# Two of the four loads of a conditioning quad moved behind the first result gathers, and its last products behind the second tile

## The reference, cut to what matters

```python
mod = (silu_c @ w_ada[i] + b_ada[i])[:, None, :]          # six vectors of 1024: shift, scale, gate, twice
h = _modulate(_rmsnorm(x, g_attn[i]), sh_a, sc_a)         # the same for the context with its own c
q, k, v = _split_qkv(h, w_qkv[i])
...
x = x + gt_a * (o @ w_o[i])
hf = _modulate(_rmsnorm(x, g_ffn[i]), sh_f, sc_f)
y = _hier_moe(tokens, w_group[i], ..., w_gate[i], w_up[i], w_down[i])
x = x + gt_f * y
```

## Time and profile before

| | us |
|---|---|
| median of 3 runs | 2221.47 |
| lowest and highest of them | 2219.11, 2228.01 |
| the profiled execution's own time | 2219.71 |
| its span in the trace | 2217.5 |
| PE busy | 1898.6 |
| DVE, ACT, POOL busy | 639.1, 400.2, 134.7 |

### The profile page before, as it was taken

How to read it: one execution, slowest core, us unless ns; L and a number is a source line. 1 busy time by engine, 2 the same in 40 slices (tenths; PEclk the granted TensorE clock), 3 DMA queues, 4 the chain that set the end, 5 groups by cost and what they waited for, 6 DMA issues and landing times.

```text
span 2217.5 us, 19432 instructions
## 1 busy us (share of the span) xinstructions
PE 1898.6 (86%) x7753; PEld 874.6 (39%) x7753; DVE 639.1 (29%) x1436; ACT 400.2 (18%) x821; POOL 134.7 (6%) x182
## 2 busy tenths in 40 slices
PE   6999968878787777886978778785999998999998
PEld 2445444323332323453323323331445553445553
DVE  1257553000000006765200000002353332362432
ACT  2146301000000012251100000001221220122220
POOL 1000002000000002001000000000100000100000
PEclk8999988999888988997999999997999999999999
DMA  9766248999999998424999999995733333533331
GB/s 368 291 259 251 99 161 334 427 427 426 427 426 424 426 397 331 160 98 151 410 426 427 427 426 427 424 419 202 247 116 123 123 114 131 200 115 115 114 114 57
DMA packets 103245, 612.13 MB, mean 276 GB/s; under 512 B 12986, under 2 KB 15306, under 8 KB 71788
## 3 DMA queue, kind: packets, MB, share of 16 engines
q1 hardware_dynamic: 85696, 572.52, 63.9%
q0 software_dynamic: 16880, 36.20, 4.8%
q10 hardware_dynamic: 576, 2.10, 0.3%
HBM read 597.43 MB, written 33.62 MB: 285 GB/s over the span
## 4 chain that ended last, share of the span: by engine, by line
PE 59%; DMA 31%; DVE 6%; ACT 1%; issue 1%; POOL 0%; SPq 0%; DVEq 0%; POOLq 0%; ACTq 0%
DMA ring<-in_w_up 24%; PE bank L706 14%; PE bank L925 12%; PE bank L786 6%; PE bank L939 5%; DMA big<-in_w_up 4%; PE bank L1003 4%; PE bank L1155 2%; PE bank L850 2%; PE bank L662 2%; PE bank L559 1%; PE bank L650 1%; PE bank L545 1%; DMA ring<-in_w_qkv 1%; DMA xl<-in_x 1%
## 5 line engine op out<-in xcount | busy, mean ns | idle before, releaser
L706 PE MATMUL bank<-ring,big 128*64 128x512 f32 x2656 | 742.5, 640 | 147.5 <-DMA ring<-in_w_gate 50.8
L706 PEld LDWEIGHTS bank<-ring,big 128*64 128x64 f32 x2656 | 247.3, 147 | 543.5 <-issue 512.0
L925 PE MATMUL bank<-ring,big 128*128 128x512 f32 (+1 forms) x640 | 282.2, 590 | 0.0
L706 PE MATMUL bank<-big 128*64 128x512 f32 x416 | 200.3, 638 | 19.6 <-DMA ring<-in_w_gate 9.5
L2010 DVE TENSOR_TENSOR big<-big,bank 128x512 f32<-128x512 f32 x32 | 22.0, 688 | 603.2 <-PE bank L706 603.2
L925 PEld LDWEIGHTS bank<-ring,big 128*128 128x128 f32 x640 | 117.5, 190 | 126.2 <-issue 126.1
L786 PE MATMUL bank<-ring,big 128*128 128x512 f32 x320 | 141.4, 601 | 2.5 <-ACT big L1199 2.1
L939 PE MATMUL bank<-ring,big 128*128 128x512 f32 x256 | 113.3, 601 | 1.7 <-issue 1.7
L1173 ACT ACTIVATE big<-bank 128x512 f32<-128x512 f32 (+1 forms) x86 | 48.2, 576 | 348.2 <-PE bank L786 101.7
L2016 DVE COPY big<-bank 128x512 f32<-128x512 f32 x32 | 22.1, 692 | 260.5 <-PE bank L706 260.5
L706 PEld LDWEIGHTS bank<-big 128*64 128x64 f32 x416 | 58.7, 146 | 84.2 <-issue 79.7
(11 more groups left out here) (371 smaller groups left out, 1824.6 us busy)
## 6 DMA issues: line engine op xcount, KB each, us to landing
ring<-in_w_up SPq DMA_DIRECT2D x56, 2048.0 KB, 23.4
ring<-in_w_down SPq DMA_DIRECT2D x56, 2048.0 KB, 24.7
ring<-in_w_gate SPq DMA_DIRECT2D x54, 2048.0 KB, 23.5
ring<-in_w_in SPq DMA_DIRECT2D x26, 2048.0 KB, 7.9
ring<-in_w_ada SPq DMA_DIRECT2D x24, 2048.0 KB, 7.8
big<-in_w_gate SPq DMA_DIRECT2D x10, 2048.0 KB, 21.2
big<-in_w_up SPq DMA_DIRECT2D x8, 2048.0 KB, 26.2
big<-in_w_down SPq DMA_DIRECT2D x8, 2048.0 KB, 24.3
```

The source lines that it names most:

```text
L706: ins = nc.tensor.matmul(bank[half * CAP:(half + 1) * CAP, :], lhs[:, k, half * CAP:(half + 1) * CAP], w[:, k * step + c0:k * step + c0 + ...
L925: ins = nc.tensor.matmul(u[:, 0:cols], HT2[:, k, tile * P:(tile + 1) * P], w[:, 0:KD * cols].rearrange("p (k n) -> p k n", k=KD)[:, k, :], ...
```

## The change

Three things move; nothing is added or left out.

- The list of weights: of layer 1's quad 4 only pieces 0 and 1 stand ahead of the three qkv pieces; pieces 2 and 3 stand behind them. SP has loads of two pieces instead of four to issue before it waits for tile 1's gathers (`s_yg[1]` at 32), and five instead of three behind that wait.
- PE: `fill_step(4, 4..7)`, half of the quad's products, moves from before tile 0's turn to behind `qkv_tile(1)`.
- DVE: `filled(4)` moves from between tile 1's modulation and the combining of tile 2 to the head of its work on tile 2.

```diff
-            put_quad(0 if layer == 0 else 4)
+            if layer == 0:
+                put_quad(0)
+            else:
+                put_quad(4, range(2))
             for c in range(3):
                 put(("qkv", layer, c), kmajor(t["w_qkv"][layer], c * 512, 512))
+            if layer == 1:
+                put_quad(4, range(2, 4))
...
-                for k in range(KD):
+                for k in range(4 if last else KD):
                     fill_step(4 if last else 0, k)
...
                     if tile < NT:
                         qkv_tile(tile)
+                    if last and tile == 1:
+                        for k in range(4, KD):
+                            fill_step(4, k)
                     if 0 <= tile - 2 < LAT:
                         qr_tile(tile - 2)
...
                     for tile in range(first, first + 2):
                         modulated_half(layer, tile)
-                    if last and first == 0:
-                        filled(4)
...
                 for tile in range(NT):
+                    if last and tile == 2:
+                        filled(4)
                     dve.wait_ge(s_outA, marks["qkv", layer, tile])
...
-                    for _ in range(4):
+                    for _ in range(2):
                         load(n)
                         n += 1
                     sp.wait_ge(s_yg[1], 32)
-                    for _ in range(3):
+                    for _ in range(5):
                         load(n)
                         n += 1
```

More of the change, by code:

```diff
@@ L373, in kmajor, with put_quad @@
             return w.rearrange("(k p) n -> p k n", p=P)[:, :, c0:c0 + n]
-        def put_quad(q):
+        def put_quad(q, items=range(KD // 2)):
             layer, c = QUADS[q]
-            for i in range(KD // 2):
+            for i in items:
                 put(("ada", q, i), kmajor(t["w_ada"][layer], c * 512, 4 * 512)[:, 2 * i:2 * i + 2, :])
```

## The result

The changed kernel took a median of 2227.01 us in 20 runs (2220.02 to 2234.76), the kernel before 2220.92 in 20 runs beside it (2216.52 to 2228.01). The ratio is 1.0024 [1.0014, 1.0033], or +5.3 us (+3.1 to +7.3): within the half per cent, but on the slow side of it. The forecast was 2222.9, a change of +1.4 us.

The account below looks back on a forecast made before the run. Bound before layer 1's attention: first the store and gathers, with nobody computing on the path, then PE with DVE touching it. -4.8 + 6.2 = +1.4 us on 2219.71 gives 2221.1, plus 1.8 a median of 2222.9; range 2217 to 2230.

Parts of the forecast that it names:

- The gain: Between layer 0's last store and layer 1's first gather: two withdrawn 2 MB loads give 4.8 us, bounded by 0 and 4.8.
- The first rival: At the last store: it is hardly helped, 0 to 2.4 us gained, median 2225.3 to 2227.7; chance 0.13.
- DVE's and PE's steps: Before quad 5's products: moved products cost DVE 3.3 us, `filled(4)` adds 2.9 us, together 6.2 us.
- The contact of the two engines at 919.3: At tile 2's rotated queries: DVE ends 0.05 us before PE needs its work, so neither has slack.
- Its distance stays: Second qkv piece, behind tile 1's gathers: its 17.90 us landing time was to stay unchanged.
- The clock: PE's clock falls at the wait before quad 5's products; price 1.7 us, median 2224.6; chance 0.12.
- Quad 5's last piece: Within quad 5's products: lands in time, 1.8 us to spare; rival has it late, +9.7 us, median 2231.2; chance 0.05.
- The bias: Quad 5's bias load on POOL: issue ends at 926.1, DVE wants it at 935.3, 9 us later.
- the three signs of being wrong: First gather moves under 3 us, PE waits within quad 5's products, or DVE's bias step is behind another wait.
- The sum: Stretch from last store to layer 1's attention: -4.8 + 6.2 = +1.4 us, median 2222.9; forecast chance 0.6.

Follow-up runs that it names:

- the small ones: 16 matmuls of 8 columns added ahead of quad 4's first half of products, against the changed kernel; ratio 1.002 [1.0005, 1.0034].

## Why the prediction was right in its range and short in its size

**The gain: right.** 4.8 us expected, 4.7 to 5.2 measured. From the store to the first gather it is 8.6 to 9.2 us in all five traces with the old loads, whatever the steps, and 3.8 to 4.5 in all nine without them. The store's own landing went from 8.27 to 3.55 us. So the loads held the store. The trace has a mark for each of the 16 shares in which a transfer lands, and it shows that a few shares made the difference, as the slow engines of the earlier trace rows would: in the kernel before 12 of the store's marks were set within 4.9 us and the last four only after 7.9 to 8.3; in the changed kernel 14 were set within 2.7. The Trainium skill, "DMA: Bandwidth & Descriptors", section "Queues, rings and completion order", has an engine's completion mark wait for its earlier writes. By that rule the store should land much sooner without the loads, and in this the trace agrees, with 3.55 us against 8.27. But the store did not wait for the loads' end: it landed at 835.4 and the second load only at 838.5, 21.0 us after its own issue at 817.4 (the 21.0 of the earlier trace rows is that load's alone). How the two shared the engines until then no run shows. The first rival, at most 2.4 us of gain, is out. The median alone could not have told: the measured 2227.0 lies within that rival's 2225.3 to 2227.7, and the stated range, 13 us wide, would have held a change of nothing as well. Being inside it says little; the times in the stretch are what bears the sum out or not.

**DVE's and PE's steps: right, 0.4 us small.** 6.2 expected, 61.43 - 54.79 = 6.64 measured: 3.06 for DVE's step instead of 2.9 (I left out the idle time at its edges), and 3.6 for PE's products, of which I had let 0.23 vanish in DVE's distance to the keys. The contact of the two engines at 919.3 was real: the wait is 3.02 us with and without PE's part.

**"Its distance stays": this is the step that failed.** I wrote that the second qkv piece's "distance stays, since the two extra loads are queued behind the three qkv pieces". The reason given holds, since holding them back changes nothing; the conclusion doesn't. The piece took 17.86 to 18.26 us in the four traces with all 64 products ahead of the first tile, and 19.24 to 19.52 in the nine with half of them there. Of that, +1.0 us reached the path. Excluded by runs: the extra loads (held back, still 19.24), the order of the loads (19.52 with the old one), DVE's step (17.92 where it alone is moved, 19.45 where it alone stays), and the number of PE's instructions (19.45 with the small ones). It goes with how long PE works there: with the half computed twice it is 18.14.

The traces say more. In all fourteen, 15 of the piece's 16 landing marks are set by 18.3 to 18.7 us after SP's first qkv issue. In the nine late traces the sixteenth follows 1.0 to 1.6 us behind the others, in the five early ones within 0.2 us. So one share of the piece is late, and the rest is where it was. And in each late trace a packet of instructions passes meanwhile. The queues of the changed kernel, from 859 to 862 us, in the piece's transfer:

```profile
q1 hardware_dynamic: 302, 0.62, 53.4%
q0 software_dynamic: 164, 0.56, 48.2%
q8 instruction: 1, 0.02, 2.2%
```

The packet has 16 KB and takes 1.03 to 1.05 us of one engine (2.2% of 16 engines in 3 us). It lies 14.0 to 15.3 us behind SP's first qkv issue in every late trace, and 6.0 to 8.7 us ahead of it in every early one. The doubled half moved it from behind the issue to ahead of it, and the late share was gone; the small products moved neither. This fits a packet that holds up one share of the piece for about its own length. Which engine carried the packet the trace doesn't tell, so this last link is an inference.

**The clock: underrated.** I gave it 0.12. It fell behind the 3.02 us wait in four of eight traces that have it, and cost 1.5 to 2.9 us (the last part of the table, 14.20 against 12.67 us in the changed kernel). My reason, that 3.08 us had once left it up, was one case where both happen.

**Quad 5's last piece and the bias.** The piece isn't waited for, but it has about 1.0 us to spare and not 1.8: issued at 924.06, it takes 8.78 us where I took 7.8, and PE wants it at 928.51 + 0.75 x 7.05 = 933.8. The spare time comes from PE's 3.02 us wait for DVE: take that away and 2.07 us of the piece show. None of the three signs of being wrong that I had named appeared; none of them looked at the qkv piece. The bias isn't late either; POOL of the changed kernel:

```profile
918.70 2.12 POOL L2368 DMA_DIRECT2D mod_d<-big  x4 [63.61 <-DVE small L1506]
922.15 2.22 POOL L2331 DMA_DIRECT2D big<-in_b_ada  x4 [1.34 <-DMA mod_d<-big]
```

Its issue ends at 924.37 and DVE wants it at 936.79, 12.4 us later where I had 9.

**The sum.** 1.4 forecast, 3.4 in the mean of the traces, 4.9 to 5.3 in the three timings (the ratios times 2221). Of the 2.0 us between forecast and traces, 1.0 is the piece, 0.5 the clock in one trace of three, and 0.4 the steps. The last 1.8 us between traces and timings lie within every interval (the lowest begins at +2.0, the highest at +3.1) but all three centres are on one side; the clock may fall oftener than in my three traces, which would give 1.0 us if it fell every time at the price of 1.5, and this is argued, not shown. As well it may be scatter: behind the attention, where the code is the same, twelve traces range from 1282.9 to 1288.2 us.

## What to carry to other kernels

A transfer on the path should not be issued behind megabytes of loads that nobody needs yet: two loads fewer gave 4.8 us here, and that gain was real and stayed. It was spent because what was moved out of an idle stretch was put where two engines touch, PE's 3.6 us and DVE's 3.1 us one behind the other; first look for a place with cover, and then for what the old wait had hidden (here a load, 2.07 us). And don't carry a transfer's duration over when the work beside it changes, even if the queue ahead of it doesn't.

## What I had not expected of the hardware

The landing of a 2 MB load moved by 1.3 us with the length of PE's work, though its neighbours in the queues were the same: one of its 16 shares was late, in just the traces in which a 16 KB packet of instructions passed at that time. Behind a wait of PE of 3.02 us the granted clock stayed at 1.00 in four traces and fell to 0.50 in four others; of the three of the changed kernel alone, it fell in one. And the place of the last store, at the end of the same instructions, scatters over 8 us from trace to trace, more than the whole effect of this change.
